# Two output projections: last blocks regrouped by token halves, one more pair of weight buffers, and a later wait for low parts

## The chip, the cores and the metric

The kernel runs on one core of a Trainium2 chip. The metric is the device time of one execution in microseconds (us); lower is better. Three runs of the kernel before gave 897.86, 897.89 and 898.0 us, a median of 897.89.

## The reference

Two transformer blocks in float32 on 256 tokens of width 1024. The first has a gated recurrent mixer and a latent attention, the second four attention mixers. What matters here is the same shape twice: the mixers' result goes through an output projection, a normalised residual is added, the sum is normalised again, and a gated feed-forward layer follows.

```
mixed = (gate_a * y_a + gate_b * y_b) @ w_out
h = h + rms_norm(mixed, mix_post_g)
u = rms_norm(h, ffn_pre_g)
gt, up = split(u @ w_ffn_in)
h = h + rms_norm((silu(gt) * up) @ w_ffn_out, ffn_post_g)
```

The second block has `mix @ w_out_2` (1024 x 1024) in the same place and a feed-forward layer with a short convolution after it.

## The kernel before

**Weights.** Each float32 number is used as a high part and a low part. Weights come from memory in slabs of 1 MB (two units of 128 x 1024 each) into three raw buffers. A step `split` makes a unit's parts (L1376, L1702, L2286): the high part is a copy into a buffer `wh` on ACT or DVE, the low part is raw minus high into `wl` on DVE or POOL. A string `MADE` (L421) names the engines of every unit. A split may start when its slab has landed and when the unit that held the buffer pair before has been used by TensorE (`opened`, L858). The planner (L390) gives each unit a buffer pair: four pairs always, eight in the feed-forward stretches. SP loads the next slab after both units of a slab have both their parts (L2369).

**Order.** Every engine walks the same list of steps, `ORDER`, and runs its own share of each in order. The list is woven from a main row and jobs by strings, `MIX` (L424): a dot takes the next main slot, a letter the next step of that job. `LATE` (L437) takes the low part of a few units out of its split and places it right behind another step.

**The stretch that is changed.** It occurs twice, as `out1` and `out2`. Here is `out1`:

- The projection has eight blocks of 128 input rows, one unit of weights each: units 76 to 83. A block takes 12 matmuls of 128x512: two token halves c, two column halves h, three products each (x high by w high, x high by w low, x low by w high). `down` (L906) makes them; before the three products it waits for both parts of the unit.
- The first four blocks are done whole, for both token halves (steps `down`). The last four, the tail (L1115), are done by token half and column half: `tail(0,0)` runs blocks 4 to 7 for c=0, h=0, then come `tail(0,1)`, `tail(1,0)` and `tail(1,1)`. So token half 0 is complete when half of the tail is still to be done. In `tail(0,0)` of `out1` alone the last block waits for the high part first and for the low part just ahead of the product that needs it.
- For each token half a chain runs beside it (`chains`, L207): `post` (ACT squares each column half and sums, L1564), `gain` (DVE, L2029), `res` (DVE adds the residual, L2044), `norm` (ACT), `scaled` (ACT and DVE, L1591 and L2057), then `turn` (eight transposes on TensorE) and eight steps `op` (ACT writes the high part of an operand, DVE the low part, L1413 and L1755).
- `gemm0` (L1000) is the first work that needs the chain of half 0: 32 matmuls of 128x256 with the high parts of units 84 to 87 (the first two tiles of the gate and of the up matrix) on token half 0. It waits for both parts of each unit. `gemm1` (L1013) adds the products for token half 1 and those with the low parts.
- In the order of the steps, `post(1,1)` and `gain(1,1)` stand ahead of `turn` and `op` of half 0; `scaled` of half 1, then `turn` of half 1, the split of unit 88 (its copy on DVE) and `op` of half 1 follow each other behind `gemm0`.
- `LATE` places the low part of unit 87 (DVE) behind `norm` of half 0.

In `out2` the units are 172 to 179 for the projection, 180 to 183 for `gemm0`, and 183 is the late one; 184 is split behind `turn` of half 1.

Of the kernel before, what the change touches and what calls it, by code (L numbers as in the profile page):

```python
# [7 lines left out]
FR = mybir.dt.float32r  # L8
U8 = mybir.dt.uint8
ACT = mybir.ActivationFunctionType  # L10
# [11 lines left out]
NUNREAD = 13  # L22
NBASE = 4
NWIDE = 8
SPLIT_TILES = 2
SLABW = 2048
IN1 = dict(hq=0, hf=1024, hi=2048, hg=3072, cq=4096, ckv=4352, kpe=4608, gate=4672)
# [69 lines left out]
def rng(o, n=128):  # L97
    return list(range(o, o + n))
# [108 lines left out]
def chains(name, x):  # L207

    return [[("post", name, c, 0), ("gain", name, c, 0), ("post", name, c, 1), ("gain", name, c, 1), ("res", name, c)]
            + ([("norm", name, c), ("scaled", name, c), ("turn", x, c)] + [("op", x, c, z) for z in range(8)] if x else [])  # L210
            for c in range(2)]


def segments():
# [7 lines left out]
    def down_tail(name, order):  # L222

        w, _, kt = DOWN[name]
        units = p.weights(("tail", name), [(w, 128 * k, rng(128 * j)) for k in order[-4:] for j in range(8)])
        return [[("tail", name, c, h)] for c in range(2) for h in range(2)], units

    def refill(units, first):

        early.extend(first)  # L230
        behind.extend(units)
        return [("open", u) for u in first] + [("behind", u) for u in units]
# [70 lines left out]
    def ffn(name, gate, up, x, nt, down, order, before):  # L303

        tail, units = down_tail(down, order)
        first = p.next_unit()
        main = before + tail
        late = []
        for i in range(SPLIT_TILES):
            for t in (gate, up):  # L310
                wn, cols = WCOLS[t](i)
                step = ("gemm", t, i, 0, 8)
                p.slot(step, [(wn, 128 * k, cols) for k in range(8)], *([("hidden", name, i)] if t == up else []))
                late += p.take()
        main.append([("gemm0", gate, up)])
        late[1].insert(2, late[0].pop())
        late[3] += [late[1].pop(), late[2].pop()]
        late[3].append(late[3].pop(2))
        main += [[("gemm1",) + s[0][1:3]] + s[1:] for s in late]
        segs.append((down, main, [*chains(down, x), refill(units, list(range(first, first + NWIDE - NBASE)))]))  # L320
        for i in range(SPLIT_TILES, nt):
            p.slot(("gemm", gate, i, 0, 8), [(WCOLS[gate](i)[0], 128 * k, WCOLS[gate](i)[1]) for k in range(8)])
            held = [p.slots[-1].pop()] if name == "ffn2" and i == nt - 2 else []
            p.slot(("gemm", up, i, 0, 8), [(WCOLS[up](i)[0], 128 * k, WCOLS[up](i)[1]) for k in range(8)],
                   ("hidden", name, i), *held)
            if i >= LAG:
                p.wide(("down", name, i - LAG), DOWN[name][0], i - LAG, [rng(128 * j) for j in range(8)])
        segs.append((None, p.take(), []))
        return first

    for n in range(8):
        p.tile("yb", n)
    for k in range(4):
        p.wide(("down", "out1", k), "w_out", k, [rng(128 * j) for j in range(8)])
    wide = [(ffn("ffn1", "g1", "u1", "x2", HID1, "out1", list(range(8)), p.take()), 0)]

# [20 lines left out]
    for n in range(2):  # L357
        p.tile("mq", n, True)
        p.tile("mk", n, True)
    for k in range(4):  # L360
        p.wide(("down", "out2", KORD2[k]), "w_out_2", KORD2[k], [rng(128 * j) for j in range(8)])

    jobs = [[("cmp_in",)] + [("cmp_hid", q) for q in range(4)] + [("cmp_act",), ("cmp_kv",), ("cmp_score",), ("cmp_prob",),
# [23 lines left out]


    count = -(-len(p.blocks) // 16) * 2
    last, place, prior, after = {b: -NWIDE + b for b in range(NWIDE)}, [], [], {}  # L390
    for u in range(count):
        n = NWIDE if any(a <= u < b for a, b in wide) else NBASE
        b = min(range(n), key=lambda b: (last[b], b)) if u >= NBASE else u
        place.append(b)
        prior.append(last[b] if last[b] >= 0 else None)
        if last[b] >= 0 and u not in early:
            after.setdefault(last[b], []).append(u)
        last[b] = u
# [10 lines left out]
    def names(steps):  # L409
# [14 lines left out]
MIX = {  # L424
    "scan": "..abc.aabc..bb.c..ab.bc...a.b.b..cc...bcb.c..a..cc...bc.b.ca.bbcd.c..cbcbad.bd.c.e.b.ecf.ef.f.f.f",
    "latent": "..a......aaaaaaaa................bc....b.fgc.b..f.c.g..de.b.cf...d.gf.e.hi.dg.h.e.d..ie.h..i.h..i",
    "out1": "............c.caac..aaacabab.bbaaaaaa.baaabbbcbbbbbbbbccc....",
    "ffn1": "..aaaaac..acaba......aaaaaaaa....bbbbccbb......b.bbbb...bbbb............",
    "maps": "...a.....acbabcbc..cc.bbb.ede.eed.ecag.agcdgcggadc.b.bfcgbefdc.ab.dgfbe.dbhffbbhhhfa.ccccf.igecbeif."
            "gahf.ddib.b.bbigchijbjj..cbhcibchkhajkhcikkhcjbiijbcijkijkcijg.kjjkk.ggkkij.k.",  # L430
    "out2": "c.caac..aaacabab.bbaaaaaa.baaabbbcbbbbbbbbccc....",
    "ffn2": "aaaaa..bb.bbb.",
}
SEGMENTS, BLOCKS, BLOCK_AT, PLACE, PRIOR, OPENS, CLOSE = segments()
NSLAB = -(-len(BLOCKS) // 16)
ORDER = [s for key, main, jobs in SEGMENTS for s in (weave(main, jobs, MIX[key]) if key else flat(main))]
LATE = {87: ('norm', 'out1', 0), 183: ('norm', 'out2', 0), 43: ('decay', 0, 6), 54: ('evac', 'qpe', 3), 154: ('scaled', 'ffn1', 0)}  # L437
for _u, _s in LATE.items():
    ORDER.insert(ORDER.index(_s) + 1, ("low", _u))
BEHIND = {("cmp_score",): (171,), ("exp", ("moba", 0)): (174,), ("join", 5): (177,),  # L440
# [12 lines left out]
LO = {u: MAKERS[MADE[u]][0] for u in range(2 * NSLAB)}  # L453
TAIL_AT = {}
for _n, (_, _, _kt) in DOWN.items():
    _ks = (KORD2 if _n == "out2" else list(range(_kt)))[-4:]
    TAIL_AT.update({(_n, _k): BLOCK_AT["tail", _n] + 8 * _i for _i, _k in enumerate(_ks)})
LAST_JOIN = [s for s in ORDER if s[0] == "join"][-1]

# [123 lines left out]
def program(nc, dr):  # L583
    ctx = ExitStack()
    with ctx:  # L585
        def sb(name, cols, dt=FP):
            return ctx.enter_context(nc.sbuf_tensor(name, [128, cols], dt))
# [24 lines left out]

        with nc.sbuf_tensor("FA", [128, NFA], FP) as FA:
            pass
        sb("FA_low", 10672)
        for i in range(NBASE, NWIDE):
            WH.append(sb(f"wh{i}", 1024, FR))
            WL.append(sb(f"wl{i}", 1024, FR))
        banks = Banks([ctx.enter_context(nc.psum_tensor(f"pb{i}", [128, 512], FP)) for i in range(8)])


# [236 lines left out]
        def opened(e, u):  # L858

            if PRIOR[u] is not None:  # L860
                e.wait_ge(*pe.at(("used", PRIOR[u])))
            if PLACE[u] >= NBASE and u < OPENS[0] + NWIDE - NBASE:
                e.wait_ge(*dve.at(("mx", "l", 7)))
                e.wait_ge(*act.at(("mx", "h", 7)))
            elif PLACE[u] >= NBASE and OPENS[1] <= u < OPENS[1] + NWIDE - NBASE:
                e.wait_ge(*pe.at(LAST_JOIN))


# [13 lines left out]
        def tensor(e):  # L882
# [53 lines left out]
            for step in ORDER:  # L936
# [63 lines left out]
                elif kind == "gemm0":  # L1000
                    src = SRC[a[0]][0]
                    tiles = [(t, i) for i in range(SPLIT_TILES) for t in a]
                    for k in TURNED[src, 0]:
                        e.wait_ge(*act.at((src, "h", k, 0)))
                        e.wait_ge(*dve.at((src, "l", k, 0)))
                        for t, i in tiles:
                            first = k == TURNED[src, 0][0]
                            b = bank(("gemm", t, i), RINGA[t]) if first else banks.of(("gemm", t, i))
                            both = b.rearrange("p (a t) -> p a t", a=2)[:, :, 0:128]
                            u, o = divmod(BLOCK_AT["gemm", t, i, 0, 8] + k, 8)  # L1010
                            unit(u)
                            e.matmul(both, whi(u, o), OPERAND[src][:, k, :, 0:128], start=first, stop=False)
                elif kind == "gemm1":  # L1013
                    name, n = a
# [3 lines left out]
                    for k in TURNED[src, 1]:  # L1018
                        e.wait_ge(*act.at((src, "h", k, 1)))
                        e.wait_ge(*dve.at((src, "l", k, 1)))  # L1020
                        for t in tiles:
                            use = ("gemm", t, n)
                            b = banks.of(use)
                            both = b.rearrange("p (a t) -> p a t", a=2)[:, :, 128:256]
                            u, o = divmod(BLOCK_AT["gemm", t, n, 0, 8] + k, 8)
                            last = k == TURNED[src, 1][-1]
                            e.matmul(both, whi(u, o), OPERAND[src][:, k, :, 128:256], start=False, stop=False)
                            m = e.matmul(b[:, 0:256], wlo(u, o), operand(src, k, 0), start=False, stop=last)
                            if last:
                                m.then_inc(*pe.up(("used", u), use))  # L1030
# [83 lines left out]
                    m.then_inc(*pe.up(step, ("used", u)))  # L1114
                elif kind == "tail":  # L1115
                    name, c, h = a
                    ks = (KORD2 if name == "out2" else list(range(DOWN[name][2])))[-4:]
                    runs = [(h, k) for k in ks]
                    if name == "ffn2" and c == 0:
                        runs = [(j, k) for j in (0, 1) for k in ks[:-1] if h == 0] + [(h, ks[-1])]  # L1120
                    if name == "ffn1" and c == 1:
                        runs = [(j, k) for k in ks[:-1] for j in (0, 1) if h == 0] + [(h, ks[-1])]
# [247 lines left out]
        def scalar(e):  # L1370
# [3 lines left out]
            for step in ORDER:  # L1374
# [189 lines left out]
                elif kind == "post":  # L1564
                    name, c, h = a
                    if c == h == 0:
# [1 line left out]
                        e.activation(stat(("one", name)), stat(("one", name)), ACT.Sqrt)  # L1568
                    s2 = stat(("post_ss", name, c), 2)
                    e.wait_ge(*pe.at(("tail", name, c, h)))  # L1570
                    e.activation(fa(6144 + 512 * (2 * c + h), 512), acc(name, c, h)[:, :], ACT.Square,
                                 accum_out=s2[:, h:h + 1]).then_inc(*act.up(step))
                    banks.ended(("acc", name, c, h), act.now())
                    if h:
# [916 lines left out]
```

## Time and profile before

| what | value |
|---|---|
| median of three runs | 897.89 us |
| the profiled execution's own time | 897.94 us |
| span of its trace | 896.1 us |
| TensorE (PE) busy | 884.4 us, 99% |
| DVE busy | 667.4 us, 74% |
| ACT busy | 466.3 us, 52% |
| granted TensorE clock, mean | 0.999 |

A timeline row gives the start (us from the span's start), how long, the engine, the line of the kernel, the operation, what it writes and reads, how many instructions are merged in the row, and in brackets the engine's idle time before it with what ended it. All engine calls go through helpers, so L528 is any matmul, L531 any transpose, L534 any ACT instruction, L537 a DVE or POOL operation on two tensors, L543 a DVE operation on two tensors and a scalar, L552 a copy. PEld is the loading of the stationary operand. Matmuls overlap: rows of full rate follow each other faster than each one lasts.

### The profile page before, as it was taken

The page shows a single profiled execution, that of the slowest core. Times are in us where ns is not written, and L with a number is a line of the kernel's source. Part 1 is how long each engine was busy: PE and PEld are TensorE (multiplying, and loading weights), DVE is VectorE, ACT ScalarE, POOL GpSimd, SP SyncE. Part 2 cuts the span into 40 slices and gives each one's busy share as a digit, 9 for nine tenths or more (in the row PEclk, how much of TensorE's full clock was granted, in tenths as well). Part 3 has the DMA queues.
Part 4 walks back from the last instruction along what each step waited for, and adds up shares of the span by engine and source line. Part 5 has one row for each costly group of instructions (what it writes and reads, how often), then busy time and mean ns, then how long its engine had stood idle before and what let it go on. Part 6 is the DMA issues. An engine that isn't in the chain of part 4 may idle for free.

```text
span 896.1 us, 16529 instructions
## 1 busy us (share of the span) xinstructions
PE 884.4 (99%) x6641; PEld 782.7 (87%) x6641; DVE 667.4 (74%) x1253; ACT 466.3 (52%) x940; POOL 200.4 (22%) x113
## 2 busy tenths in 40 slices
PE   9999999999999999999999999999999999999997
PEld 8879999989999798888888899977888888888886
DVE  7745987586447877786666767768888788788885
ACT  7444336665344774444444657866553545543443
POOL 4123421531132120553214522230001111210100
PEclk9999999999999999999999999999999999999999
DMA  8356453153424746555564374215354465465441
GB/s 331 114 184 234 140 174 112 48 212 142 142 96 145 278 163 236 188 196 187 187 219 169 124 247 165 97 48 211 142 222 161 182 213 204 152 230 188 174 156 48
DMA packets 23180, 153.66 MB, mean 171 GB/s; under 512 B 2864, under 2 KB 3248, under 8 KB 5568
## 3 DMA queue, kind: packets, MB, share of 16 engines
q1 hardware_dynamic: 22384, 150.44, 46.8%
q0 software_dynamic: 576, 2.10, 0.6%
q8 instruction: 53, 0.87, 0.4%
q14 instruction: 23, 0.19, 0.1%
q10 hardware_dynamic: 144, 0.07, 0.0%
HBM read 151.28 MB, written 1.05 MB: 170 GB/s over the span
## 4 chain that ended last, share of the span: by engine, by line
PE 96%; DVE 2%; ACT 1%; issue 1%; DVEq 0%; ACTq 0%
PE pb L528 94%; PE pb L531 2%; ACT FA L534 1%; DVE FA L537 0%; DVE wl L537 0%; ACT R L534 0%; DVE X L543 0%; DVE wh L552 0%; DVE FA L546 0%; ACT wh L534 0%; DVE FA L540 0%; DVE st L540 0%; DVE st L555 0%; DVEq L585 0%; DVE FA L543 0%
## 5 line engine op out<-in xcount | busy, mean ns | idle before, releaser
L528 PE MATMUL pb<-R,wh 128*128 128x256 f32 (+2 forms) x2224 | 545.5, 325 | 3.3 <-DVE R L543 2.0
L528 PE MATMUL pb<-R,wl 128*128 128x256 f32 (+1 forms) x1512 | 420.0, 281 | 0.0
L528 PEld LDWEIGHTS pb<-R,wh 128*128 128x128 f32 x2224 | 369.5, 188 | 43.3 <-ACT R L534 3.4
L537 DVE TENSOR_TENSOR wl<-raw,wh 128x1024 fp32r<-128x1024 f32 (+1 forms) x207 | 273.3, 1344 | 76.6 <-ACT wh L534 74.8
L537 POOL TENSOR_TENSOR wl<-raw,wh 128x1024 fp32r<-128x1024 f32 (+1 forms) x71 | 173.4, 2445 | 581.5 <-ACT wh L534 427.4
L528 PEld LDWEIGHTS pb<-R,wl 128*128 128x128 f32 x1512 | 283.4, 188 | 1.7
L534 ACT ACTIVATE wh<-raw 128x1024 fp32r<-128x1024 f32 (+1 forms) x223 | 226.1, 1044 | 52.0 <-PE pb L528 36.9
L528 PE MATMUL pb<-wh,R 128*128 128x512 f32 (+1 forms) x704 | 227.1, 389 | 0.1
L528 PEld LDWEIGHTS pb<-wh,R 128*128 128x128 f32 x704 | 131.7, 188 | 31.1 <-issue 1.7
L534 ACT ACTIVATE FA<-pb 128x256 f32<-128x256 f32 (+7 forms) x240 | 93.2, 411 | 118.4 <-PE pb L528 103.2
L528 PE MATMUL pb<-wl,R 128*128 128x512 f32 (+1 forms) x352 | 135.5, 385 | 0.0
L534 ACT ACTIVATE FA<-FA 128x256 f32<-128x256 f32 (+4 forms) x69 | 28.0, 406 | 138.9 <-DVE FA L543 118.8
L537 DVE TENSOR_TENSOR FA<-FA 128x256 f32<-128x256 f32 (+7 forms) x120 | 71.6, 621 | 10.1 <-ACT FA L534 2.9
L528 PEld LDWEIGHTS pb<-wl,R 128*128 128x128 f32 x352 | 66.1, 188 | 11.6
L537 DVE TENSOR_TENSOR FA<-pb,FA 128x256 f32<-128x256 f32 (+1 forms) x132 | 56.5, 434 | 24.8 <-ACT FA L534 24.3
L534 ACT ACTIVATE R<-FA 128x256 fp32r<-128x256 f32 (+1 forms) x66 | 28.3, 431 | 52.2 <-DVE FA L537 52.2
L528 PE MATMUL pb<-FA 128*32 128x16 f32 (+6 forms) x1360 | 54.0, 217 | 0.3 <-ACT FA L534 0.2
L528 PEld LDWEIGHTS pb<-FA 128*32 128x32 f32 (+3 forms) x1360 | 47.1, 130 | 7.2 <-issue 2.0
L552 DVE CAST wh<-raw 128x1024 fp32r<-128x1024 f32 (+1 forms) x55 | 42.3, 771 | 13.3 <-PE pb L528 12.7
L537 DVE TENSOR_TENSOR R<-FA,R 128x256 fp32r<-128x256 f32 (+1 forms) x59 | 27.4, 468 | 26.2 <-ACT R L534 26.1
L543 DVE SCALAR_TENSOR_TENSOR FA<-FA,sm 128x255 f32<-128x255 f32 x64 | 31.0, 484 | 2.3
L534 ACT ACTIVATE FA<-FA,st 128x256 f32<-128x256 f32 (+2 forms) x65 | 29.3, 454 | 5.2 <-DVE st L546 4.9
(127 smaller groups left out, 434.6 us busy)
## 6 DMA issues: line engine op xcount, KB each, us to landing
raw<-in_w SPq DMA_DIRECT2D x137, 1024.0 KB, 4.8
X<-in_x SPq DMA_DIRECT2D x2, 512.0 KB, 4.1
raw<-in_w SPq DMA_DIRECT2D x2, 512.0 KB, 6.8
post<-in_ffn_post SPq DMA_DIRECT2D x2, 512.0 KB, 4.3
post<-in_w POOLq DMA_DIRECT2D x2, 512.0 KB, 4.9
FA<-in_w POOLq DMA_DIRECT2D x2, 512.0 KB, 8.0
out<-X SPq DMA_DIRECT2D x4, 256.0 KB, 2.0
cst<-in_cst SPq DMA_DIRECT2D x1, 822.5 KB, 12.6
```

The source lines that it names most:

```text
L528: return self.real.matmul(*a, **k) if self.real else self
L531: return self.real.transpose(*a, **k) if self.real else self
L534: return self.real.activation(*a, **k) if self.real else self
L537: return self.real.tensor_tensor(*a, **k) if self.real else self
L543: return self.real.scalar_tensor_tensor(*a, **k) if self.real else self
L552: return self.real.tensor_copy(*a, **k) if self.real else self
```

## The change

- The tail of `out1` and `out2` has five blocks in place of four (units 79 to 83, and 175 to 179); three blocks in place of four are done whole.
- For token half 0 of these tails, all blocks but the last are run for h=0, then for h=1, and then the last block for h=0 and for h=1. Half 1 stays as it was, with five blocks.
- The last unit of the tail (83, 179) is held in a ninth pair of buffers, at a place of its own; its split stands ahead of the others that are opened there. The next units (88 to 91, 184 to 187) follow 79 to 82 and 175 to 178 in the four base pairs.
- `gemm0` waits for the high parts only; `gemm1` waits for both.
- The low parts of units 87 and 183 are moved from behind `norm` of half 0 to behind `scaled` of half 1.
- The place where `post` writes its squares (not read again) is moved, to leave room for the ninth pair.

```diff
+ASIDE = 8
+TAILS = dict(out1=5, ffn1=4, out2=5, ffn2=4)
...
-        units = p.weights(("tail", name), [(w, 128 * k, rng(128 * j)) for k in order[-4:] for j in range(8)])
+        units = p.weights(("tail", name), [(w, 128 * k, rng(128 * j)) for k in order[-TAILS[name]:] for j in range(8)])
...
-        segs.append((down, main, [*chains(down, x), refill(units, list(range(first, first + NWIDE - NBASE)))]))
+        segs.append((down, main, [*chains(down, x), refill(units[:-1], list(range(first - 1, first + NWIDE - NBASE)))]))
...
-    for k in range(4):
+    for k in range(8 - TAILS["out1"]):
         p.wide(("down", "out1", k), "w_out", k, [rng(128 * j) for j in range(8)])
...
-    last, place, prior, after = {b: -NWIDE + b for b in range(NWIDE)}, [], [], {}
+    last, place, prior, after = {b: -NWIDE + b for b in range(NWIDE + 1)}, [], [], {}
...
+        if any(u == a - 1 for a, _ in wide):
+            b = ASIDE
...
-    "out1": "............c.caac..aaacabab.bbaaaaaa.baaabbbcbbbbbbbbccc....",
+    "out1": "...........cc.caac..aaacabab.bbaaaaaa.baaabbbcbbbbbbbbccc....",
...
-    "out2": "c.caac..aaacabab.bbaaaaaa.baaabbbcbbbbbbbbccc....",
+    "out2": "cc.caac..aaacabab.bbaaaaaa.baaabbbcbbbbbbbbccc....",
...
-LATE = {87: ('norm', 'out1', 0), 183: ('norm', 'out2', 0), 43: ('decay', 0, 6), 54: ('evac', 'qpe', 3), 154: ('scaled', 'ffn1', 0)}
+LATE = {87: ('scaled', 'out1', 1), 183: ('scaled', 'out2', 1), 43: ('decay', 0, 6), 54: ('evac', 'qpe', 3), 154: ('scaled', 'ffn1', 0)}
...
-            elif PLACE[u] >= NBASE and OPENS[1] <= u < OPENS[1] + NWIDE - NBASE:
+            elif PLACE[u] >= NBASE and OPENS[1] - 1 <= u < OPENS[1] + NWIDE - NBASE:
                 e.wait_ge(*pe.at(LAST_JOIN))
...
                             u, o = divmod(BLOCK_AT["gemm", t, i, 0, 8] + k, 8)
-                            unit(u)
+                            e.wait_ge(*(act if HI[u] == "act" else dve).at(("hi", u)))
...
                             u, o = divmod(BLOCK_AT["gemm", t, n, 0, 8] + k, 8)
+                            unit(u)
...
-                    if name == "ffn2" and c == 0:
+                    if name != "ffn1" and c == 0:
                         runs = [(j, k) for j in (0, 1) for k in ks[:-1] if h == 0] + [(h, ks[-1])]
...
-                    e.activation(fa(6144 + 512 * (2 * c + h), 512), acc(name, c, h)[:, :], ACT.Square,
+                    e.activation(fa(2048 + 1024 * c + 512 * h, 512), acc(name, c, h)[:, :], ACT.Square,
```

## Rows read from the trace of the kernel before

**Rows 1.** The page, part 1: busy time and share of the span, number of instructions.
```profile
PE 884.4 (99%) x6641; PEld 782.7 (87%) x6641; DVE 667.4 (74%) x1253; ACT 466.3 (52%) x940; POOL 200.4 (22%) x113
```

**Rows 2.** Windows at the two sites: window and length, busy us (count) of PE, PEld, DVE, ACT, POOL.
```profile
309.90:317.70 7.80, 6.39 (x49) 5.62 (x49) 6.73 (x21) 6.72 (x22) 0.74 (x1) 1.00 0.58 203
...
619.30:627.00 7.70, 6.18 (x50) 5.41 (x48) 6.35 (x19) 6.50 (x21) 0.76 (x1) 1.00 0.54 204
```

**Rows 3.** Timeline of PE at out1: first and last projection matmul, transposes, gemm0, gemm1.
```profile
287.96 0.40 PE L528 MATMUL pb<-wh,R 128*128 128x512 f32 x1
...
309.55 0.39 PE L528 MATMUL pb<-wh,R 128*128 128x512 f32 x1
...
310.17 1.07 PE L531 MATMUL pb<-cst,FA 128*128 128x128 f32 x8 [0.23 <-DVE st L540]
...
312.11 4.28 PE L528 MATMUL pb<-R,wh 128*128 128x256 f32 x32 [0.88 <-DVE R L543]
...
317.71 0.36 PE L528 MATMUL pb<-R,wh 128*128 128x256 f32 x1 [0.28 <-ACT R L534]
```

**Rows 4.** Timeline of PE at out2: last projection matmul, transposes, gemm0.
```profile
619.01 0.39 PE L528 MATMUL pb<-wh,R 128*128 128x512 f32 x1
...
619.24 1.03 PE L531 MATMUL pb<-cst,FA 128*128 128x128 f32 x8
...
621.38 4.24 PE L528 MATMUL pb<-R,wh 128*128 128x256 f32 x32 [1.11 <-DVE R L543]
```

**Rows 5.** Timeline of ACT and DVE at out1: post(0,1), scaled, post(1,1), op high, op low.
```profile
304.54 0.60 ACT L534 ACTIVATE FA<-pb 128x512 f32<-128x512 f32 x1 [0.92 <-PE pb L528]
...
309.57 0.71 ACT L534 ACTIVATE FA<-X,st 128x512 f32<-128x512 f32 x1
...
310.18 0.58 ACT L534 ACTIVATE FA<-pb 128x512 f32<-128x512 f32 x1
...
311.08 2.33 ACT L534 ACTIVATE R<-pb,sm 128x128 fp32r<-128x128 f32 x8
...
311.63 1.38 DVE L543 SCALAR_TENSOR_TENSOR R<-pb,sm,R 128x128 fp32r<-128x128 f32 x5
```

**Rows 6.** Timeline of ACT at out2: post(1,1).
```profile
619.44 0.60 ACT L534 ACTIVATE FA<-pb 128x512 f32<-128x512 f32 x1 [0.17 <-PE pb L528]
```

**Rows 7.** Timeline of ACT, DVE and PE at out1: making units 81 and 82, block 3's matmuls.
```profile
294.95 2.68 DVE L537 TENSOR_TENSOR wl<-raw,wh 128x1024 fp32r<-128x1024 f32 x1 [0.68 <-ACT wh L534]
...
296.41 1.06 ACT L534 ACTIVATE wh<-raw 128x1024 fp32r<-128x1024 f32 x1 [1.49 <-PE pb L528]
...
297.55 1.21 DVE L537 TENSOR_TENSOR wl<-raw,wh 128x1024 fp32r<-128x1024 f32 x1
...
297.96 0.62 PE L528 MATMUL pb<-wh,R 128*128 128x512 f32 x2
```

**Rows 8.** Timeline at out2: low parts of 178 and of 179, 180; PE in tail(0,0).
```profile
606.03 1.23 DVE L537 TENSOR_TENSOR wl<-raw,wh 128x1024 fp32r<-128x1024 f32 x1
...
608.95 2.36 DVE L537 TENSOR_TENSOR wl<-raw,wh 128x1024 fp32r<-128x1024 f32 x2
...
609.84 0.91 PE L528 MATMUL pb<-wh,R 128*128 128x512 f32 x2
...
610.25 0.19 PEld L528 LDWEIGHTS pb<-wh,R 128*128 128x128 f32 x1 [0.45 <-DVE wl L537]
```

**Rows 9.** Timeline of DVE at out1: low part of 87, copy of 88, op low.
```profile
308.20 1.22 DVE L537 TENSOR_TENSOR wl<-raw,wh 128x1024 fp32r<-128x1024 f32 x1
...
316.19 0.69 DVE L552 CAST wh<-raw 128x1024 fp32r<-128x1024 f32 x1
...
317.21 2.16 DVE L543 SCALAR_TENSOR_TENSOR R<-pb,sm,R 128x128 fp32r<-128x128 f32 x8 [0.33 <-ACT R L534]
```

**Rows 10.** Slab loads (page, part 6), and ACT's copy of unit 92 (timeline).
```profile
raw<-in_w SPq DMA_DIRECT2D x137, 1024.0 KB, 4.8
...
325.80 1.05 ACT L534 ACTIVATE wh<-raw 128x1024 fp32r<-128x1024 f32 x1
```

More of the change, by code:

```diff
@@ L359, in segments @@
         p.tile("mk", n, True)
-    for k in range(4):
+    for k in range(8 - TAILS["out2"]):
         p.wide(("down", "out2", KORD2[k]), "w_out_2", KORD2[k], [rng(128 * j) for j in range(8)])
@@ L426 @@
     "latent": "..a......aaaaaaaa................bc....b.fgc.b..f.c.g..de.b.cf...d.gf.e.hi.dg.h.e.d..ie.h..i.h..i",
-    "out1": "............c.caac..aaacabab.bbaaaaaa.baaabbbcbbbbbbbbccc....",
+    "out1": "...........cc.caac..aaacabab.bbaaaaaa.baaabbbcbbbbbbbbccc....",
     "ffn1": "..aaaaac..acaba......aaaaaaaa....bbbbccbb......b.bbbb...bbbb............",
     "maps": "...a.....acbabcbc..cc.bbb.ede.eed.ecag.agcdgcggadc.b.bfcgbefdc.ab.dgfbe.dbhffbbhhhfa.ccccf.igecbeif."
-            "gahf.ddib.b.bbigchijbjj..cbhcibchkhajkhcikkhcjbiijbcijkijkcijg.kjjkk.ggkkij.k.",
-    "out2": "c.caac..aaacabab.bbaaaaaa.baaabbbcbbbbbbbbccc....",
+            "gahf.ddib.b.bbigchijbjj..cbhcibchkhajkhcikkhcjbiijbcijkijkcijg.kjjkk.ggkkij.k",
+    "out2": "cc.caac..aaacabab.bbaaaaaa.baaabbbcbbbbbbbbccc....",
     "ffn2": "aaaaa..bb.bbb.",
@@ L455 @@
 for _n, (_, _, _kt) in DOWN.items():
-    _ks = (KORD2 if _n == "out2" else list(range(_kt)))[-4:]
+    _ks = (KORD2 if _n == "out2" else list(range(_kt)))[-TAILS[_n]:]
     TAIL_AT.update({(_n, _k): BLOCK_AT["tail", _n] + 8 * _i for _i, _k in enumerate(_ks)})
@@ L614, in program @@
             pass
-        sb("FA_low", 10672)
+        sb("FA_low", 6144)
+        aside = sb(f"wh{ASIDE}", 1024, FR), sb(f"wl{ASIDE}", 1024, FR)
+        sb("FA_mid", 10672 - 8192)
         for i in range(NBASE, NWIDE):
@@ L618, in program @@
             WL.append(sb(f"wl{i}", 1024, FR))
+        WH.append(aside[0])
+        WL.append(aside[1])
         banks = Banks([ctx.enter_context(nc.psum_tensor(f"pb{i}", [128, 512], FP)) for i in range(8)])
@@ L1116, in tensor @@
                     name, c, h = a
-                    ks = (KORD2 if name == "out2" else list(range(DOWN[name][2])))[-4:]
+                    ks = (KORD2 if name == "out2" else list(range(DOWN[name][2])))[-TAILS[name]:]
                     runs = [(h, k) for k in ks]
-                    if name == "ffn2" and c == 0:
+                    if name != "ffn1" and c == 0:
                         runs = [(j, k) for j in (0, 1) for k in ks[:-1] if h == 0] + [(h, ks[-1])]
```

## The prediction, before the changed kernel ran

> **What bounds the kernel now.** First the page's busy times: TensorE (PE) is busy 884.4 of the 896.1 us of the span [rows 1]. So the total can only change by what PE waits, 11.7 us in all, and what the change can give or cost is read from PE's waits at its two sites. The windows show them: from the end of each projection to `gemm1`, PE is idle 7.80 - 6.39 = 1.41 us at out1 and 7.70 - 6.18 = 1.52 us at out2 [rows 2]; elsewhere around the tails it runs on. PE's timeline tells where: after the last projection matmul it waits 0.23 us for the transposes at out1 (nothing at out2), then 0.88 and 1.11 us for the first operand of `gemm0`, then 0.28 us for `gemm1` [rows 3, 4]. At out2 there is one more wait, inside the tail: a pair of matmuls that elsewhere takes 0.62 us [rows 7] takes 0.91, released by the low part of unit 179 [rows 8]. The reader should keep that PE's work is the same before and after: the change only moves waits.
>
> **The change, part by part.** Times below are counted on PE; the 96 projection matmuls of out1 start at 287.96, the last at 309.55, so one every (309.55 - 287.96) / 95 = 0.227 us.
>
> 1. *Five blocks in the tail give half 0 more cover: 6 matmuls, 1.36 us.* What can that shorten? At out2 the chain of half 0 was already in time (the transposes follow at once) and `gemm0` still began 621.38 - 619.01 = 2.37 us after the last matmul's start [rows 4]. Rows 6 say why: ACT starts `post(1,1)` at 619.44, as soon as that matmul is done, and in ACT's and DVE's order `post` and `gain` of the second half stand ahead of the `op` steps that `gemm0` needs. More cover does not move that. At out1 the same stretch took 312.11 - 309.55 = 2.56 us [rows 3], since ACT was busy with `scaled` (309.57, 0.71 us) and came to `post(1,1)` at 310.18; `op` began at 311.08 and 311.63 [rows 5]. With more cover that falls to out2's figure: **-0.19 us** at out1, 0 at out2. Ends: -1.1 us each if the `op` steps got ahead of `post(1,1)`, 0 if ACT is as late as now. The new order for half 0 eats most of the cover: `post(0,0)` and `post(0,1)` come 0.68 us apart, with the copy of unit 86 between them (1.06 us, as the copy of 82 takes [rows 7]), so I place `post(0,1)` at about 304.85 instead of 304.54 [rows 5] and the end of `scaled` at about 310.5. By part 2 the tail ends there too, so it hides; without part 2 the 0.2 to 0.3 us would show.
>
> 2. *The weights of the tail are wanted sooner.* Before, block 3 was done whole while the next units were being made. Now `tail(0,0)` runs through units 79, 80, 81 and 82 in twelve matmuls. Unit 82 goes into the buffer of unit 78, which block 2 leaves just before the tail begins. ACT copies its high part from 296.41, and DVE's low part runs from 297.55 to 298.76 [rows 7]; nothing ahead of these changes, so they stay. Now three products of unit 82 are the tail's 10th to 12th: the 46th matmul, second of the pair at 297.96, thus due at 298.19 [rows 7]. What a low part costs from its end to the first matmul is seen at unit 179: it ended at 608.95 + 1.22 = 610.17, and the matmul, second of the pair of 0.91 that began at 609.84, ran from 610.75 - 0.39 = 610.36, 0.19 later [rows 8]. So PE starts at 298.95: **+0.76 us** at out1. (Unit 81, whose low part took 2.68 us and ends near 297.6 [rows 7], costs a third of that on the way, and it is in the 0.76.) At out2 the wait for 179 goes, since the ninth pair is free earlier: 0.62 - 0.91 = -0.29. Late next is 178: its low part ends at 606.03 + 1.23 = 607.26 [rows 8], PE could go at 607.45; it would be wanted 12 matmuls ahead of the place that 179 would have without its wait, 609.84 + 0.23 - 12 x 0.227 = 607.34. So +0.11, together **-0.18 us** at out2. Ends: 0 if ACT and DVE were sooner (no row shows it), 1.1 at out1 if 82's low part is slowed by half as much as 81's was.
>
> PE's weight loads: at unit 179 the wait stands on the load, which began at 610.25, 0.11 before its matmul [rows 8]. The Trainium skill (TensorE: Matmul & The Clock Gate, step-by-step, the first phase) says that PE can pull weight loads ahead of running matmuls; the operand loaded here is not the late one, so by that rule the load would be done already, the 0.76 would be 0.65 and the sum below 1.90 instead of 2.01. The trace differs at the one place where this wait occurs, so I stay with its row.
>
> 3. *`gemm0` waits for high parts alone.* That wait removes nothing: the low part of 87 ended at 308.20 + 1.22 = 309.42 [rows 9], 2.7 us ahead of `gemm0`. It only allows part 4. The waits added to `gemm1` find 84 to 86 long made and 87 done before DVE starts the operands: 0.
>
> 4. *The low parts of 87 and 183 move behind `scaled` of half 1.* This leaves a place where DVE has no PE waiting on it (part 1) for one where it has. There DVE runs `scaled`, the copy of 88 (316.19), then `op` from 317.21, and PE starts `gemm1` 0.50 us later, at 317.71 [rows 9, 3]. Now 1.22 us of low part stand ahead of the copy; back to back such operations come every 2.36 - 1.22 = 1.14 us [rows 8]. DVE was idle 0.33 us just ahead of `op` [rows 9] and that absorbs some: 1.14 - 0.33 = **+0.81 us**, at each site (out2 has the same steps in the same order). Queued behind it on DVE are the copy of 88 (POOL waits for it) and all eight `op` steps, with PE behind them. Ends: 0 if it hides, 1.22 if nothing is absorbed. SP waits for 87's low part before it loads the slab with unit 92: issued about 318 + 1.4 instead of 309.5, landed 4.8 us later, near 324, while ACT copies 92 at 325.80 + 1.4 [rows 10]. The load of the gains queued behind it is for the feed-forward's end. No cost.
>
> 5. *The new place of the squares and the extra pair* add no instruction: 0.
>
> **Sum.** out1: -0.19 + 0.76 + 0.81 = 1.38. out2: -0.18 + 0.81 = 0.63. Together +2.01 us on the profiled execution's 897.94 (span 896.1 and 1.8 around it), 899.95; the median of the runs is 0.05 lower, so **899.9 us**. PE is not idle again long enough behind either site to win it back.
>
> **The rivals.**
> - *The cover was what was missing (faster).* If half 0's chain, and not `post(1,1)`, sets the start of `gemm0`, then 1.36 us of cover closes the waits of 0.23, 0.88 and 1.11 us, the 0.29 goes too, and the moved low parts hide: -2.5, **895.4**. For it: DVE works almost without a break up to `gemm0` of out1. Against it: out2, where the chain was in time and the wait was longest [rows 4, 6]. It decides if `op` starts before `post(1,1)` is over.
> - *The moved low parts hide*, because the operands wait for something later than DVE: 2.01 - 1.62 = +0.39, **898.3**. Against it: PE follows DVE's `op` by 0.5 us at both operands of out1 [rows 3, 5, 9].
> - *The weights are in time* (part 2 costs nothing at out1). Then ACT's chain, 0.2 to 0.3 us later, shows in place of the -0.19: 0.25 + 0.81 - 0.18 + 0.81 = +1.7, **899.6**.
> - *A further wait*: with the two `post` close together, half 0's chain ends later than my 310.5 and the transposes wait as well, by as much as a copy of 1.06 us: +3.1, **901.0**.
>
> **How the numbers follow.** Chances: forecast 0.52, cover 0.08, hidden 0.17, weights in time 0.13, further wait 0.10. A measurement of this kernel can tell about 0.2%, 1.8 us, from no change, and the forecast lies just past that; I give four fifths of it to slower (its terms can be 0.3 too large), the rest to same. Slower: 0.42 + 0.10 = 0.52. Same: 0.10 + 0.17 + 0.13 = 0.40. Faster: 0.08. The range reaches down to the case of the hidden low parts, 898.2, and up to the forecast with nothing absorbed on DVE (1.22 for 0.81, twice), 900.8, and most of the further wait: 898.2 to 900.9.
>
> **What would show it.** Right: PE idle in `tail(0,0)` of out1 ahead of the third unit, released by DVE; `gemm0` still 2.4 us behind the last projection matmul at both sites; a 1.22 us low part between `scaled` and the copy of 88, and 1.1 us of idle ahead of `gemm1` instead of 0.28; no wait for 179. Wrong: `gemm0` within 1.5 us of the tail's end, or `gemm1` as close behind the transposes as before.

## The result, and the profile after

After: 899.94 us, median of 12 runs (899.62 to 901.24). Before: 898.07 us, median of 12 (897.65 to 898.45). The ratio is 1.0022, 95% interval 1.0013 to 1.0031: slower by 1.87 us, and the whole interval lies above 1. The 0.2% that the prediction took for the least difference that can be told lies inside it. The forecast was 899.9, +2.01.

The profiled execution of the changed kernel took 899.62 us, span 897.8. Its start-up was shorter: out1 begins at 287.57 instead of 287.96 [rows 3]. So the spans differ by 1.7 us only, and all that follows is counted from the beginning of a site. The new code shifts the lines by 4: L532 is a matmul, L535 a transpose, L538 ACT, L541 a two-tensor operation, L547 one with a scalar, L556 a copy, L571 a DMA.

The page of the kernel after, part 1 (engine, busy us, share, number of instructions):

```profile
PE 884.3 (98%) x6641; PEld 782.1 (87%) x6641; DVE 666.5 (74%) x1253; ACT 466.5 (52%) x940; POOL 200.1 (22%) x113
```

PE does the same work as before [rows 1]; what changed is its waits. The timeline of PE after, first out1, then out2:

```profile
296.90 0.95 PE L532 MATMUL pb<-wh,R 128*128 128x512 f32 x2
...
297.92 0.40 PE L532 MATMUL pb<-wh,R 128*128 128x512 f32 x1
298.52 0.47 PE L532 MATMUL pb<-wh,R 128*128 128x512 f32 x1 [0.20 <-DVE wl L541]
298.83 0.39 PE L532 MATMUL pb<-wl,R 128*128 128x512 f32 x1
...
303.86 0.63 PE L532 MATMUL pb<-wh,R 128*128 128x512 f32 x2
...
309.41 0.62 PE L532 MATMUL pb<-wh,R 128*128 128x512 f32 x2
...
310.11 0.40 PE L532 MATMUL pb<-wh,R 128*128 128x512 f32 x1
310.34 1.03 PE L535 MATMUL pb<-cst,FA 128*128 128x128 f32 x8
312.49 4.28 PE L532 MATMUL pb<-R,wh 128*128 128x256 f32 x32 [1.11 <-DVE R L547]
...
318.80 0.36 PE L532 MATMUL pb<-R,wh 128*128 128x256 f32 x1 [0.99 <-DVE R L547]
...
606.50 0.48 PE L532 MATMUL pb<-wh,R 128*128 128x512 f32 x1
...
608.44 0.72 PE L532 MATMUL pb<-wh,R 128*128 128x512 f32 x2
...
620.29 0.40 PE L532 MATMUL pb<-wh,R 128*128 128x512 f32 x1
620.53 1.03 PE L535 MATMUL pb<-cst,FA 128*128 128x128 f32 x8
622.67 4.28 PE L532 MATMUL pb<-R,wh 128*128 128x256 f32 x32 [1.11 <-DVE R L547]
...
628.98 0.35 PE L532 MATMUL pb<-R,wh 128*128 128x256 f32 x1 [0.99 <-DVE R L547]
```

For the comparison, four rows of the kernel before that were not shown yet: the timeline of PE, two of token half 1 at out1, the first matmul of the last 60 of out2's projection (606.50 above), and `gemm1` of out2.

```profile
303.43 0.61 PE L528 MATMUL pb<-wh,R 128*128 128x512 f32 x2
...
308.87 0.61 PE L528 MATMUL pb<-wh,R 128*128 128x512 f32 x2
...
605.17 0.48 PE L528 MATMUL pb<-wh,R 128*128 128x512 f32 x1
...
626.99 0.35 PE L528 MATMUL pb<-R,wh 128*128 128x256 f32 x1 [0.28 <-ACT R L534]
```

The reader is to see three things, the rows of before being [rows 3, 4]:

- *In the tail of out1 PE stands.* The pair at 296.90 takes 0.95 us instead of 0.62; its second matmul is the first of unit 81. The matmul at 298.52 waits for unit 82. It is the 46th; it was due 298.19 - 287.96 = 10.23 us after the first [rows 7, 3], and came 298.52 - 287.57 = 10.95 after it, 0.72 late. Before, there was no wait here.
- *`gemm0` comes no nearer to the end of the projection.* 312.49 - 310.11 = 2.38 us at out1 (before 2.56), 2.38 at out2 (before 2.37).
- *`gemm1` waits 0.99 us where it waited 0.28.* From `gemm0` to `gemm1` it is 6.31 us at both sites (before 5.60 and 5.61).

DVE's timeline after at out1: low parts of 81 and 82, `gain(1,1)`, `op` of half 0, `scaled` of half 1, low part of 87, copy of 88, `op` of half 1.

```profile
294.56 3.81 DVE L541 TENSOR_TENSOR wl<-raw,wh 128x1024 fp32r<-128x1024 f32 x2 [0.67 <-ACT wh L538]
...
311.33 0.69 DVE L541 TENSOR_TENSOR FA<-pb,post 128x512 f32<-128x512 f32 x1 [0.94 <-ACT FA L538]
312.01 1.38 DVE L547 SCALAR_TENSOR_TENSOR R<-pb,sm,R 128x128 fp32r<-128x128 f32 x5
...
316.17 0.49 DVE L544 TENSOR_SCALAR FA<-X,st 128x512 f32<-128x512 f32 x1
316.57 1.22 DVE L541 TENSOR_TENSOR wl<-raw,wh 128x1024 fp32r<-128x1024 f32 x1
317.70 0.69 DVE L556 CAST wh<-raw 128x1024 fp32r<-128x1024 f32 x1
318.31 2.15 DVE L547 SCALAR_TENSOR_TENSOR R<-pb,sm,R 128x128 fp32r<-128x128 f32 x8
```

The low part of 87 (316.57) stands between `scaled` and the copy of 88, and behind them `op` of half 1 starts at 318.31; `gemm1` follows it by 0.49 us, as it did before [rows 9, 3].

ACT's timeline after at out1: `post(0,1)`, `scaled` of half 0, `post(1,1)`, `op` of half 0.

```profile
304.44 0.59 ACT L538 ACTIVATE FA<-pb 128x512 f32<-128x512 f32 x1
...
309.49 0.71 ACT L538 ACTIVATE FA<-X,st 128x512 f32<-128x512 f32 x1
...
310.54 0.60 ACT L538 ACTIVATE FA<-pb 128x512 f32<-128x512 f32 x1 [0.34 <-PE pb L532]
...
311.46 2.33 ACT L538 ACTIVATE R<-pb,sm 128x128 fp32r<-128x128 f32 x8
```

`post(1,1)` now waits for PE (0.34 us) instead of for ACT's own `scaled` [rows 5]: half 0's chain is in time, and `op` of half 0 still stands behind `post(1,1)`. `post(0,1)` itself came where the prediction put it: 304.44, with the 0.39 us of shorter start-up 304.83 for its 304.85.

### The profile page after: what moved, and what is told of

The parts are those of the page before. It is cut to its first block, busy times and chain, and to the rows that moved or that the text cites. A ratio compares the mean times of both kernels' runs of the same rounds, so it can differ in the third digit from the quotient of the medians.

```text
span 897.8 us, 16529 instructions
## 1 busy us (share of the span) xinstructions
PE 884.3 (98%) x6641; PEld 782.1 (87%) x6641; DVE 666.5 (74%) x1253; ACT 466.5 (52%) x940; POOL 200.1 (22%) x113
## 4 chain that ended last, share of the span: by engine, by line
PE 92%; DVE 5%; ACT 2%; issue 1%; DMA 1%; SPq 0%; DVEq 0%; ACTq 0%
PE pb L532 90%; PE pb L535 2%; DVE wl L541 1%; DVE R L547 1%; ACT wh L538 1%; DVE FA L541 1%; ACT FA L538 1%; DMA X<-in_x 1%; DVE FA L547 0%; DVE X L547 0%; ACT R L538 0%; DVE FA L544 0%; DVE FA L550 0%; DVE wh L556 0%; DVE st L559 0%
## 5 line engine op out<-in xcount | busy, mean ns | idle before, releaser
L532 PE MATMUL pb<-R,wh 128*128 128x256 f32 (+2 forms) x2224 | 545.7, 325 | 4.8 <-DVE R L547 4.2
L532 PE MATMUL pb<-R,wl 128*128 128x256 f32 (+1 forms) x1512 | 420.0, 281 | 0.0
L532 PEld LDWEIGHTS pb<-R,wh 128*128 128x128 f32 x2224 | 369.6, 188 | 44.7 <-ACT R L538 5.0
L541 DVE TENSOR_TENSOR wl<-raw,wh 128x1024 fp32r<-128x1024 f32 (+1 forms) x207 | 273.1, 1343 | 76.5 <-ACT wh L538 75.0
L541 POOL TENSOR_TENSOR wl<-raw,wh 128x1024 fp32r<-128x1024 f32 (+1 forms) x71 | 173.0, 2440 | 583.6 <-ACT wh L538 426.5
L532 PEld LDWEIGHTS pb<-R,wl 128*128 128x128 f32 x1512 | 283.4, 188 | 1.7
L538 ACT ACTIVATE wh<-raw 128x1024 fp32r<-128x1024 f32 (+1 forms) x223 | 226.1, 1043 | 52.6 <-PE pb L532 37.8
L532 PE MATMUL pb<-wh,R 128*128 128x512 f32 (+1 forms) x704 | 227.6, 389 | 0.3 <-DVE wl L541 0.2
L532 PEld LDWEIGHTS pb<-wh,R 128*128 128x128 f32 x704 | 131.7, 188 | 32.2 <-issue 2.3
L538 ACT ACTIVATE FA<-pb 128x256 f32<-128x256 f32 (+7 forms) x240 | 93.5, 412 | 121.7 <-PE pb L532 106.5
L532 PE MATMUL pb<-wl,R 128*128 128x512 f32 (+1 forms) x352 | 135.6, 385 | 0.0
L538 ACT ACTIVATE FA<-FA 128x256 f32<-128x256 f32 (+4 forms) x69 | 28.0, 405 | 135.9 <-DVE FA L547 118.4
L541 DVE TENSOR_TENSOR FA<-FA 128x256 f32<-128x256 f32 (+7 forms) x120 | 70.7, 613 | 10.0 <-ACT FA L538 2.5
L532 PEld LDWEIGHTS pb<-wl,R 128*128 128x128 f32 x352 | 66.1, 188 | 11.5
L541 DVE TENSOR_TENSOR FA<-pb,FA 128x256 f32<-128x256 f32 (+1 forms) x132 | 56.6, 434 | 26.1 <-ACT FA L538 25.7
L538 ACT ACTIVATE R<-FA 128x256 fp32r<-128x256 f32 (+1 forms) x66 | 28.3, 431 | 51.8 <-DVE FA L541 51.8
L532 PE MATMUL pb<-FA 128*32 128x16 f32 (+6 forms) x1360 | 54.0, 217 | 0.3 <-ACT FA L538 0.2
L532 PEld LDWEIGHTS pb<-FA 128*32 128x32 f32 (+3 forms) x1360 | 47.1, 130 | 7.2 <-issue 2.1
L556 DVE CAST wh<-raw 128x1024 fp32r<-128x1024 f32 (+1 forms) x55 | 42.1, 768 | 12.0 <-PE pb L532 11.9
L541 DVE TENSOR_TENSOR R<-FA,R 128x256 fp32r<-128x256 f32 (+1 forms) x59 | 27.4, 468 | 26.2 <-ACT R L538 26.1
L547 DVE SCALAR_TENSOR_TENSOR FA<-FA,sm 128x255 f32<-128x255 f32 x64 | 30.9, 483 | 2.3
L538 ACT ACTIVATE FA<-FA,st 128x256 f32<-128x256 f32 (+2 forms) x65 | 29.3, 455 | 5.2 <-DVE st L550 4.9
```

Source lines behind the costliest of these rows:

```text
L532: return self.real.matmul(*a, **k) if self.real else self
L538: return self.real.activation(*a, **k) if self.real else self
L541: return self.real.tensor_tensor(*a, **k) if self.real else self
L547: return self.real.scalar_tensor_tensor(*a, **k) if self.real else self
L556: return self.real.tensor_copy(*a, **k) if self.real else self
```

## The experiments

Each was timed in five rounds beside the kernel before (898.08 us for e1 to e4, 898.07 for e5 to e8); as it came out the same each time, the times are also set against the changed kernel's 899.94.

| experiment | edit | us | ratio to before, 95% |
|---|---|---|---|
| e1_low_back | after, low parts of 87 and 183 back | 898.79 | 1.0007 (0.9998 to 1.0016) |
| e2_low_move_alone | before, only these low parts moved | 899.32 | 1.0014 (1.0005 to 1.0023) |
| e3_blocks_first | after, half 0 of the tail by blocks | 899.00 | 1.0010 (1.0002 to 1.0019) |
| e4_ops_first | after, five `op` ahead of `post(1,1)` | 900.98 | 1.0034 (1.0021 to 1.0046) |
| e5_blocks_first_low_last | e3 and the low parts behind the last `op` | 898.30 | 1.0003 (0.9994 to 1.0011) |
| e6_low_last_alone | before, low parts behind the last `op` | 898.51 | 1.0004 (0.9995 to 1.0014) |
| e7_columns_first | after, half 0 wholly by columns | 901.95 | 1.0044 (1.0032 to 1.0057) |
| e8_blocks_first_low_back | e3 and e1 together | 897.98 | 0.9998 (0.9989 to 1.0007) |

**e1: undo the move of the low parts.**

```diff
-LATE = {87: ('scaled', 'out1', 1), 183: ('scaled', 'out2', 1), ...
+LATE = {87: ('norm', 'out1', 0), 183: ('norm', 'out2', 0), ...
```

> The changed kernel with the low parts of units 87 and 183 put back behind norm of half 0. My theory (the moved low part stands on DVE ahead of the op steps of half 1 and costs PE about 0.7 us at each site): 899.94 - 1.4 = 898.5, PE's wait ahead of gemm1 back from 0.99 to 0.28 us, gemm0 still 2.4 us behind the last projection matmul. Rival (half 0's chain needs DVE free of the low part, so that moving it won as much as it cost): no faster than 899.9, and gemm0 starts later behind the tail.

Measured 898.79, 1.15 below the changed kernel. PE's timeline of e1 at out1, `gemm0` and `gemm1`:

```profile
313.07 4.28 PE L532 MATMUL pb<-R,wh 128*128 128x256 f32 x32 [1.11 <-DVE R L547]
...
318.66 0.36 PE L532 MATMUL pb<-R,wh 128*128 128x256 f32 x1 [0.28 <-ACT R L538]
```

From `gemm0` to `gemm1` it is 5.59 us again, the wait 0.28 again, and `gemm0` still waits 1.11. The move costs 6.31 - 5.59 = 0.72 us at out1, by the trace. Timed, undoing it at both sites gave 1.15 where I had expected 1.4.

**e2: make that move alone, on the kernel before** (with the waits of `gemm0` and `gemm1` that go with it).

```diff
+LATE = {87: ('scaled', 'out1', 1), 183: ('scaled', 'out2', 1), ...
...
-                            unit(u)
+                            e.wait_ge(*(act if HI[u] == "act" else dve).at(("hi", u)))
...
+                            unit(u)
```

> The kernel before with only the low parts of 87 and 183 moved behind scaled of half 1 (and gemm0 waiting for high parts alone, which that needs). My theory: two waits of 0.7 us more ahead of gemm1, less 0.2 at out1 where ACT's scaled of half 0 comes a little sooner: 898.07 + 1.2 = 899.3. Rival (the move is free, the five blocks cost all): 898.1.

Measured 899.32, +1.24. The last projection matmul and the same two rows of e2:

```profile
309.43 0.39 PE L528 MATMUL pb<-wh,R 128*128 128x512 f32 x1
...
312.00 4.28 PE L528 MATMUL pb<-R,wh 128*128 128x256 f32 x32 [1.09 <-DVE R L543]
...
318.31 0.36 PE L528 MATMUL pb<-R,wh 128*128 128x256 f32 x1 [1.00 <-DVE R L543]
```

6.31 us, as in the kernel after: this part does it by itself, without five blocks. The rival that the moved low parts hide is out. And `gemm0`, which here waits for high parts alone, starts no sooner: 312.00 - 309.43 = 2.57 us behind the last projection matmul (before 2.56). So the 0.2 us that I took off at out1 did not come, and that the time fits my 899.3 so well is in part luck: two waits of 0.71 us would make +1.42.

**e3: in half 0 of the tail, run each block for both column halves** before the next one, so that units 81 and 82 are wanted later.

```diff
-                    if name != "ffn1" and c == 0:
+                    if name == "ffn2" and c == 0:
...
+                    if name in ("out1", "out2") and c == 0:
+                        runs = [(j, k) for k in ks[:-1] for j in (0, 1) if h == 0] + [(h, ks[-1])]
```

> The changed kernel with half 0 of the two tails ordered by blocks (each block for h=0 and h=1, the last block still at the end), so that unit 82 is wanted nine matmuls later. My theory: PE's waits inside the tail (0.7 us at out1, 0.1 at out2) go, but then ACT's chain of half 0 shows at out1, since it does not move: gemm0 0.4 to 0.5 us sooner, 899.4. Rival (every wait in the tail counts in full): 899.0. Rival (the waits are no loss because half 0's chain ends last anyway): 899.9.

Measured 899.00, 0.94 below the changed kernel. The rival, that the waits for weights count in full, came out; my theory here, that part of them would come back behind half 0's chain, did not. PE's timeline of e3 at out1, transposes, `gemm0`, `gemm1`:

```profile
309.84 1.03 PE L535 MATMUL pb<-cst,FA 128*128 128x128 f32 x8
311.99 4.28 PE L532 MATMUL pb<-R,wh 128*128 128x256 f32 x32 [1.11 <-DVE R L547]
...
318.30 0.35 PE L532 MATMUL pb<-R,wh 128*128 128x256 f32 x1 [1.00 <-DVE R L547]
```

The projection runs without a wait, the transposes follow it at once, and `gemm0` waits the same 1.11 us.

**e8: e3 and e1 together**, five blocks and the ninth pair without the two costs.

> Five blocks, half 0 by blocks, low parts of 87 and 183 back behind norm of half 0: both costs that I blame are undone and the five blocks, the ninth pair and the waits stay. My theory: 899.0 - 1.15 = 897.85, about the kernel before (898.08), less the wait for 179 (0.3) and plus what the slower matmuls of half 1 take. Rival (a third cost hides in the five blocks): 898.5 or more.

Measured 897.98. The two savings add up: 899.94 - 1.15 - 0.94 = 897.85 was the sum. What is left of the change (five blocks, the ninth pair) is not to be told from the kernel before. PE's timeline of e8 at out1, last projection matmul, transposes, `gemm0`, `gemm1` (the first projection matmul is at 287.97):

```profile
309.70 0.39 PE L532 MATMUL pb<-wh,R 128*128 128x512 f32 x1
310.15 1.06 PE L535 MATMUL pb<-cst,FA 128*128 128x128 f32 x8
312.10 4.28 PE L532 MATMUL pb<-R,wh 128*128 128x256 f32 x32 [0.89 <-DVE R L547]
...
317.70 0.36 PE L532 MATMUL pb<-R,wh 128*128 128x256 f32 x1 [0.28 <-ACT R L538]
```

Here the cover stands by itself, though with half 0 in another order than in the change, and in this trace half 0's chain is not wholly in time: the transposes come 0.45 us behind the last matmul instead of 0.23. `gemm0` still comes 2.40 us behind it. From the first matmul to `gemm1` it is 29.73 us, before 29.75. So what the cover gains at `gemm0`, 0.16 us, the projection loses again, and nothing is left that can be measured.

**e4: `turn` and five `op` of half 0 ahead of `post(1,1)` and `gain(1,1)`** at both sites, the order that the forecast named as the reason for `gemm0`'s wait.

```diff
-    "out1": "...........cc.caac..aaacabab.bbaaaaaa.baaabbbcbbbbbbbbccc....",
+    "out1": "...........cc.caac..aaacabab.aaaaaabb.baaabbbcbbbbbbbbccc....",
...
```

> The changed kernel with turn and the first five op steps of half 0 ahead of post(1,1) and gain(1,1) in every engine's order. My theory (post(1,1) ahead of op sets the start of gemm0, and half 1's chain sets gemm1): gemm0 about 0.8 us sooner behind the tail, but gemm1 about 0.6 us later at each site, 899.94 + 1.2 = 901.1. Rival (the wait ahead of gemm0 is the loss, so closing it wins): 899.94 - 1.6 = 898.3.

Measured 900.98, 1.04 above the changed kernel. PE's timeline of e4 at out1 (the last projection matmul is at 310.37):

```profile
312.03 2.60 PE L532 MATMUL pb<-R,wh 128*128 128x256 f32 x20 [0.39 <-DVE R L547]
...
315.91 1.65 PE L532 MATMUL pb<-R,wh 128*128 128x256 f32 x12 [1.28 <-DVE R L547]
...
319.60 0.36 PE L532 MATMUL pb<-R,wh 128*128 128x256 f32 x1 [1.00 <-DVE R L547]
```

`gemm0` does start sooner, 1.66 us behind the last projection matmul instead of 2.38. So it is this order that sets its start. But `post(1,1)` then starts 2.14 us behind that matmul (ACT, 312.51) instead of 0.43, and the last three `op` steps stand behind it. PE stops for 1.28 us in the middle of `gemm0`, and `gemm1` comes 9.23 us behind the projection instead of 8.69. The order that makes `gemm0` wait is the better one.

**e6 and e5: the low parts behind the last `op` of half 1**, where PE should not wait for DVE: e6 on the kernel before, e5 on e3.

```diff
+LATE = {87: ('op', 'x2', 1, 7), 183: ('op', 'x4', 1, 7), ...
...
```

> The kernel before with only the low parts of 87 and 183 behind the last op step of half 1, and gemm0 waiting for high parts alone. My theory: the 0.7 us ahead of gemm1 that e2 showed are gone, since DVE reaches op as early as before; at out1 up to 0.2 us less ahead of gemm0: 897.9 to 898.1. Rival (any place behind gemm0 costs PE the same 1.2 us of DVE): 899.3.

> Five blocks, half 0 by blocks, and the low parts of 87 and 183 behind the last op step of half 1, where no operand waits for DVE. My theory: neither the waits in the tail nor the wait ahead of gemm1 are left, and half 0's chain has DVE to itself: 899.0 - 1.15 = 897.85, and a little under e8. Rival (the low part is then late for gemm1 or pushes the next splits): 898.5 or more, with PE idle in or behind gemm1.

Measured 898.51 and 898.30: neither is to be told from before, and both lie above what I expected, by 0.4 to 0.6. `gemm1` waits 0.28 in both. In e6 out1 is unharmed: `gemm1` comes 317.74 - 288.00 = 29.74 us after the first matmul (before 317.71 - 287.96 = 29.75). PE's timeline of e6: first `gemm1` of out1, then a matmul of the stage behind out2. The second fence has the same matmul in e5.

```profile
317.74 0.36 PE L528 MATMUL pb<-R,wh 128*128 128x256 f32 x1 [0.28 <-ACT R L534]
...
646.38 0.47 PE L528 MATMUL pb<-R,wh 128*128 128x512 f32 x1 [0.24 <-DVE FA L537]
```

```profile
645.76 0.47 PE L532 MATMUL pb<-R,wh 128*128 128x512 f32 x1 [0.25 <-DVE FA L541]
```

DVE's low parts of two units shortly ahead of that matmul, in e6 and, in the second fence, before:

```profile
643.53 2.36 DVE L537 TENSOR_TENSOR wl<-raw,wh 128x1024 fp32r<-128x1024 f32 x2 [0.53 <-ACT wh L534]
```

```profile
643.04 2.36 DVE L537 TENSOR_TENSOR wl<-raw,wh 128x1024 fp32r<-128x1024 f32 x2 [0.53 <-ACT wh L534]
```

The low part of 183 hides at `gemm1`, but DVE is then late: these low parts start 643.53 - 627.04 = 16.49 us behind `gemm1` of out2 (at 627.04 in e6), before 643.04 - 626.99 = 16.05. 19 us behind `gemm1` PE waits for DVE, for 0.24 us; in the kernel before, PE's timeline marks no wait from 640 to 662 us. That is what e5's rival said, only smaller. The rest lies within the intervals.

**e7: half 0 wholly by columns**, all five blocks for h=0 and then for h=1, so that the ninth pair's unit is wanted early too.

```diff
-                    if name != "ffn1" and c == 0:
+                    if name == "ffn2" and c == 0:
```

> The changed kernel with half 0 of the two tails ordered as before, all five blocks for h=0 and then all five for h=1. My theory: unit 83 is now wanted too, right behind 82 (its high part is there, its low part about 0.8 us late), and at out2 179 after 178 (about 1.2 us late), so PE waits that much more in the tails, 899.94 + 2.0 = 901.9, of which half 0's chain, begun earlier, gives nothing back. Rival (the regrouping of half 0 costs by its late post, so undoing it wins): 899.5 or less.

Measured 901.95, 2.01 above the changed kernel. PE's timeline of e7 in the two tails:

```profile
298.93 0.47 PE L532 MATMUL pb<-wh,R 128*128 128x512 f32 x1 [0.20 <-DVE wl L541]
...
300.70 0.50 PE L532 MATMUL pb<-wl,R 128*128 128x512 f32 x1 [0.38 <-DVE wl L541]
...
611.77 0.47 PE L532 MATMUL pb<-wh,R 128*128 128x512 f32 x1 [1.27 <-DVE wl L541]
```

The last unit of the tail makes PE wait at out1 (300.70) and at out2 (611.77, 1.27 us). So a unit's place in the order prices the wait, and the last block's place behind both column halves, which the change has, is what keeps unit 83 and 179 free of it. Nothing of these waits comes back at `gemm0`, whose wait stays 1.11.

No version beats the kernel before by more than the measurement can tell; e8 is the nearest.

## Why the prediction was right

The terms, each against the trace of the kernel after, counted from the beginning of its own stretch:

| term | forecast | trace |
|---|---|---|
| cover, out1 | -0.19 | 2.38 - 2.56 = -0.18 |
| cover, out2 | 0 | 2.38 - 2.37 = +0.01 |
| weights, out1 | +0.76 | 10.95 - 10.23 = +0.72 |
| rest of the projection, out1 | 0 | 22.54 - 21.59 - 0.72 = +0.23 |
| weights and projection, out2 | -0.18 | 13.79 - 13.84 = -0.05 |
| low part of 87 | +0.81 | 6.31 - 5.60 = +0.71 |
| low part of 183 | +0.81 | 6.31 - 5.61 = +0.70 |
| sum | +2.01 | +2.14 |

The spans differ by 1.7: 2.14, less 0.39 of start-up, plus 0.24 between the sites and less 0.29 behind the last one. These three are no part of the argument: the stretch between the sites takes 287.46 us before and 287.70 after, and with like edits it falls now here, now there (287.46 in e1, 287.69 in e8). So two timed kernels can differ by 0.2 to 0.3 us by such stretches alone. The medians are 1.87 apart; e1 and e3, timed, put 1.15 + 0.94 = 2.09 us on the low parts and the weights, the whole of it.

1. *Cover: right.* Five blocks brought out1 to out2's figure and no further (2.38 us also in e1 and e3; with four blocks 2.57 in e2). e4 shows the reason by moving it: with `op` ahead of `post(1,1)` `gemm0` starts 0.7 us sooner and all is slower. The rival that the cover was missing is out: in the kernel after the transposes follow at once at both sites and `gemm0` waits 1.11 us all the same, and e8, which has the cover without the two costs, is no faster than before.

2. *Weights: right, to 0.04 us.* Unit 82's low part ended 298.37 - 287.57 = 10.80 us after the first matmul, as I had it from before (298.76 - 287.96 = 10.80); PE followed by 0.15 instead of 0.19. The Trainium skill's rule (TensorE: Matmul & The Clock Gate, step-by-step, the first phase), that PE can pull weight loads ahead of running matmuls, says nothing of a load that the program places behind a wait; the prediction read it as if a load could pass that wait too, which would give 0.65. The trace shows 0.72: the load, too, waited for the low part. Timeline of the weight loads after at out1, for the first matmuls of units 81 and 82:

```profile
297.35 0.19 PEld L532 LDWEIGHTS pb<-wh,R 128*128 128x128 f32 x1 [0.49 <-ACT wh L538]
...
298.49 0.19 PEld L532 LDWEIGHTS pb<-wh,R 128*128 128x128 f32 x1 [0.61 <-issue]
```

The load for unit 82 began 0.12 us behind the low part's end, and the matmul 0.03 behind it. At unit 81 it is the same: its low part took 2.68 us from 294.56, as before [rows 7], and ended at 297.24, 0.11 ahead of the load. (The row names ACT, whose copy of 82 had ended at 297.07.)

At out2 the wait for 179 went and 178's came: the pair at 608.44 takes 0.72 instead of 0.62, +0.10 for my +0.11.

3. *The wait for high parts alone: right,* it gives nothing (e2).

4. *The moved low parts: the mechanism was right, the term was too large,* 0.81 for 0.70. What was mis-sized is the step "DVE was idle 0.33 us just ahead of `op` and that absorbs some". The low part and its spacing took 317.70 - 316.57 = 1.13, as I had it; but from the copy to `op` it was 317.21 - 316.19 = 1.02 us before [rows 9] and is 318.31 - 317.70 = 0.61 now. So 0.41 was absorbed: the 0.33 of idle time, and 0.08 because `op` now starts before the copy's 0.69 us are over.

5. *A term was missing:* besides the waits the projection runs slower, by 0.23 us at out1 and 0.14 at out2 (-0.05 where -0.29 + 0.10 = -0.19 of waits was gained). At out1 0.08 of it is the matmul behind the wait itself, which the next one follows by 298.83 - 298.52 = 0.31 us instead of 0.23; the rest is told below. So the premise that the change only moves waits did not hold wholly. Missing +0.37 and oversized +0.25 partly cancel, so the total is closer than its parts deserve, and that the median meets the forecast to 0.04 us is in part luck.

6. *A rival was priced wrongly.* For "weights in time" I let half 0's chain keep its time of day and show by 0.2 to 0.3 us. But that time was behind a tail that stood for unit 82; without the wait the chain moves forward with PE. In e3 `gemm0` waits 1.11 with the tail undisturbed, and the time is the 899.0 of waits that count in full. (e3 takes another order for half 0, so the diff's own order without waits was not tried.) The rival of a further wait is out: the transposes follow the projection at once.

*SP's queue was rightly costed at nothing.* The slab that waits for 87's low part is indeed late. SP's timeline after: that load, and the gains behind it.

```profile
317.88 0.33 SPq L571 DMA_DIRECT2D raw<-in_w  x1
318.25 0.43 SPq L571 DMA_DIRECT2D post<-in_ffn_post  x1
```

It was issued at 317.88, before at 309.51, and no row of PE waits for it afterwards.

## What to carry to other kernels

When a wait is to be closed by more work in front of it, look first at what the waiting operand is queued behind: here the second half's own `post`, which moves with the last matmul, so once the chain was in time the distance to `gemm0` stayed at 2.37 to 2.38 us, with four blocks (out2) as with five. A grouping that makes one result complete sooner asks for every operand of it sooner; set the end of each operand's making against the matmul that will want it, one by one, and the stall comes out closely (here 0.76 us for 0.72). And a step with slack where it stands (the low part behind `norm`) is only worth moving if its new place has more.

## What was not expected of the hardware

With five blocks in the tail the 512-column matmuls of half 1 follow each other more slowly, at the same granted clock (1.00 in both, the upper of its two levels). At out1 eight groups of three take 308.87 - 303.43 = 5.44 us before, 227 ns for one, and 309.41 - 303.86 = 5.55 us after, 231 ns. Out2 shows the same, 227 and 231 ns. All six experiments with five blocks have 231 (e1, e3, e4, e5, e7, e8), and the two with four have 227 (e2, e6). Over the 30 matmuls of half 1 that is 0.14 us for a site. It is not the moved low parts (e1 and e8 have them back), nor the waits in the tail (e3 and e8 have none), nor the order of half 0 (e3 and e7 have others). But every run with five blocks also has the ninth pair of buffers and the new place of the squares: which of these, or what in the longer tail, it comes from stays open, no run here separates them.
